# Moving small work between and within the engines' streams in a fused two-block layer: GDN's key decay, its triangles and right side, RG-LRU and mLSTM's second convolution

## What is computed

```python
u = rmsnorm(x, attn_norm) @ w_in          # one product for four mixers
gdn, mlstm, rglru, rwkv = split(u)
y = concat(gated_deltanet(gdn), mlstm(mlstm), rglru_block(rglru), rwkv7_time_mix(rwkv))
x = x + y @ w_out
x = x + swiglu_ffn(rmsnorm(x, ffn_norm))  # 5632 hidden
...                                       # second block: attention, memory, gated merge
```

```python
def gated_delta_rule(q, k, v, g, beta):
    g = jnp.cumsum(g, axis=-1)
    decay = jnp.exp(jnp.where(causal, g[..., :, None] - g[..., None, :], -jnp.inf))
    kb = k * beta[..., None]
    lower = jnp.tril(jnp.einsum('nbhcd,nbhsd->nbhcs', kb, k) * decay, -1)
    rhs = jnp.concatenate([v * beta[..., None], kb * jnp.exp(g)[..., None]], axis=-1)
    sol = lax.linalg.triangular_solve(lower + eye, rhs, ...)
    ...
    k_dec = k * jnp.exp(g[..., -1:] - g)[..., None]
...
def mlstm(...):
    qk = jax.nn.silu(causal_conv(qk, conv_w))        # q and k: two convolutions
...
def rglru_block(u, conv_w, conv_b, w_a, b_a, w_x, b_x, lam):
    xb = causal_conv(xb, conv_w) + conv_b
    r = sigmoid(xh @ w_a + b_a); i = sigmoid(xh @ w_x + b_x)
    log_a = -RGLRU_C * r * jax.nn.softplus(-lam)
```

## Time and profile before

| | us |
|---|---|
| median of 3 runs | 2447.65 |
| lowest, highest | 2445.69, 2447.93 |
| the profiled execution | 2449.26 |
| its span | 2447.5 |
| TensorE busy | 2408.2 (98%) |
| VectorE busy | 1412.7 (58%) |
| ScalarE busy | 1129.1 (46%) |
| GpSimd busy | 113.8 (5%) |
| mean granted clock of TensorE | 0.996 |

### The profile page before, as it was taken

The page is one execution under the profiler, slowest core; times in us unless marked ns, Lnnn a source line. Parts: engine busy times, 40 slices in busy tenths (PEclk is TensorE's granted clock), DMA queues, the critical chain, the costliest instruction groups (busy, mean ns, idle before and its releaser), DMA issues.

```text
span 2447.5 us, 34354 instructions
## 1 busy us (share of the span) xinstructions
PE 2408.2 (98%) x14480; PEld 2050.0 (84%) x14480; DVE 1412.7 (58%) x1834; ACT 1129.1 (46%) x1412; POOL 113.8 (5%) x100
## 2 busy tenths in 40 slices
PE   7999999999999999999999999999999999999998
PEld 7997999987888888888888878898888888888887
DVE  4866657776765555555555565545446645555554
ACT  6535435563454444444434464445444455444444
POOL 2100001210000000000000050000000000000000
PEclk9999999999999999999999999999999999999999
DMA  8633334645555556655555566555545544555564
GB/s 254 211 121 109 134 122 156 220 160 186 193 189 185 187 179 200 194 187 186 179 192 187 187 203 232 184 172 172 161 154 197 170 161 140 199 187 184 195 243 143
DMA packets 225641, 441.53 MB, mean 180 GB/s; under 512 B 11890, under 2 KB 28112, under 8 KB 223056
## 3 DMA queue, kind: packets, MB, share of 16 engines
q1 hardware_dynamic: 221744, 419.80, 52.2%
q0 software_dynamic: 3744, 19.53, 2.1%
HBM read 428.81 MB, written 10.49 MB: 179 GB/s over the span
## 4 chain that ended last, share of the span: by engine, by line
PE 91%; issue 4%; DVE 3%; ACT 2%; DMA 0%; POOL 0%; SPq 0%; ACTq 0%; DVEq 0%; POOLq 0%
PE ps L600 24%; PE ps L601 24%; PE ps L602 24%; PE ps L628 4%; PE ps L629 4%; PE ps L630 4%; PE ps L559 2%; PE ps L1213 1%; PE ps L1202 1%; PE ps L734 1%; DVE ringL L1874 1%; DVE AR L2348 0%; ACT ringH L1274 0%; DMA mem_hold<-memSt 0%; PE ps L818 0%
## 5 line engine op out<-in xcount | busy, mean ns | idle before, releaser
L1274 ACT CAST ringH<-raw 128x1024 fp32r<-128x1024 f32 x780 | 816.1, 1049 | 1008.1 <-PE ps L602 871.0
L1874 DVE TENSOR_TENSOR ringL<-raw,ringH 128x1024 fp32r<-128x1024 f32 x780 | 951.9, 1237 | 442.0 <-ACT ringH L1274 441.1
L600 PE MATMUL ps<-ringH,nS 128*128 128x512 f32 x1376 | 552.6, 402 | 2.3 <-DVE nS L2594 1.1
L602 PE MATMUL ps<-ringH,nS 128*128 128x512 f32 x1376 | 538.0, 391 | 0.0
L601 PE MATMUL ps<-ringL,nS 128*128 128x512 f32 x1376 | 537.8, 391 | 0.0
L628 PE MATMUL ps<-nS,ringH 128*128 128x256 f32 x1056 | 310.4, 294 | 8.4 <-DVE ringL L1874 6.9
L600 PEld LDWEIGHTS ps<-ringH,nS 128*128 128x128 f32 x1376 | 259.3, 188 | 57.2 <-DVE ringL L1874 4.3
L602 PEld LDWEIGHTS ps<-ringH,nS 128*128 128x128 f32 x1376 | 259.0, 188 | 55.5
L601 PEld LDWEIGHTS ps<-ringL,nS 128*128 128x128 f32 x1376 | 259.5, 189 | 49.2 <-issue 0.2
L629 PE MATMUL ps<-nS,ringH 128*128 128x256 f32 x1056 | 300.0, 284 | 0.0
L630 PE MATMUL ps<-nS,ringL 128*128 128x256 f32 x1056 | 299.7, 284 | 0.0
(11 more groups left out here) (413 smaller groups left out, 2135.0 us busy)
## 6 DMA issues: line engine op xcount, KB each, us to landing
raw<-in_w_in SPq DMA_DIRECT2D x189, 1024.0 KB, 5.1
raw<-in_ffn_w_gate SPq DMA_DIRECT2D x44, 1024.0 KB, 5.2
raw<-in_ffn_w_up SPq DMA_DIRECT2D x44, 1024.0 KB, 5.2
raw<-in_ffn_w_down SPq DMA_DIRECT2D x44, 1024.0 KB, 5.1
raw<-in_w_out SPq DMA_DIRECT2D x32, 1024.0 KB, 5.1
raw<-in_w_mem_kv SPq DMA_DIRECT2D x16, 1024.0 KB, 5.2
raw<-in_w_proj_a SPq DMA_DIRECT2D x8, 1024.0 KB, 5.1
raw<-in_w_proj_m SPq DMA_DIRECT2D x8, 1024.0 KB, 5.1
```

The lines of the kernel that those rows point to most:

```text
L600: mm(o, XH[:, ts(j)], WH, first, False)
L602: t_of[0] = mm(o, XL[:, ts(j)], WH, False, last)
L1274: e.copy(ringH[:, h % NSPL, 0:nh * cols], raw[:, u % NRAW, h0 * cols:(h0 + nh) * cols]).then_inc(*hi.tick(h))
L1874: tt2(ringL[:, h % NSPL, o], raw[:, u % NRAW, h0 * cols:(h0 + nh) * cols], ringH[:, h % NSPL, o].bitcast(F32), SUB).then_inc(*lo.tick(h))
```

## The change

It has these parts:

1. `norm` on ScalarE: the root comes one halt earlier.
2. `mem`: TensorE's and VectorE's `factor` for the memory's rows come one halt of one step later.
3. mLSTM's second convolution (q = 1) starts two halts later on TensorE, ScalarE and VectorE.
4. RG-LRU starts two halts later on all engines, GpSimd's products and the transfers of w2s included.
5. The split mix312 becomes mix3, run in one go, and mix1 and mix2, each with a halt after every second chunk. The w_out blocks wait for their own mixer's split.
6. GDN: Kt is scaled by ScalarE (four Copy activations with a scale) in place of VectorE; `pairs` is called for a group when its G is there; the right side of the first chunk is computed within `join`.

```diff
@@ def small_mixers(L):
     while not L.done("r0") and "gdn" not in L.open:
         yield
+    yield
+    yield
     yield from L.stage("rglru")
     yield from L.stage("xload")
...
-    L.run("mix312")
+    L.run("mix3")
     yield
+    for m in (1, 2):
+        for n, _ in enumerate(L.stage(f"mix{m}")):
+            if n % 2:
+                yield
@@ program: gates of the w_out blocks
-                  ("gdn" if m == 2 and q >= 2 else "mix312") if m else "mix0", "V")
+                  "gdn" if m == 2 and q >= 2 else f"mix{m}", "V")
@@ TensorE, mem
                 yield 2
                 yield 2
+                yield 1
                 factor("me", me_p, me_v, rm)
@@ TensorE, mlstm
-                    for _ in range(5):
+                    for _ in range(5 + 2 * q):
                         yield
@@ TensorE, gdn, product vn
                     e.wait_ge(*gd_v.at("R", ch))
+                    e.wait_ge(*gd_v.at("inv", "xt", "j"))
@@ ScalarE, norm
-                yield
                 root(nx_v, nx_a, rx)
+                yield
                 yield
@@ ScalarE and VectorE, mlstm
-                    yield
+                    for _ in range(1 + 2 * q):
+                        yield
@@ ScalarE, gdn
-                yield
-                for _ in range(4):
+                for _ in range(3):
+                    yield
+                Kt = v3(SC + 1024 * 9, 4, 128)
+                e.wait_ge(*gd_a.at("kd"))
+                for h in range(4):
+                    t = act(Kt[:, h, :], Kt[:, h, :], ACT.Copy, scale=kd[:, h:h + 1])
+                t.then_inc(*gd_a.tick("kdt"))
+                for _ in range(2):
                     yield
@@ VectorE, factor
                 e.reciprocal(r, r).then_inc(*mv.tick("r"))
+                if key == "me":
+                    yield
                 e.wait_ge(*mp.at("r"))
@@ VectorE, pairs
-                    first = [(s, bc(mask(C_M1T), 4), bc(ident, 4)) for s in (slice(0, 4), slice(4, 8))]
+                    first = [(s, bc(mask(C_M1T), 4), bc(ident, 4)) for s in (slice(4 * g, 4 * g + 4) for g in groups)]
@@ VectorE, gdn
-                e.wait_ge(*gd_a.at("kd"))
-                for h in range(4):
-                    t = tsc(Kt[:, h, :], Kt[:, h, :], kd[:, h:h + 1], None, MUL)
-                t.then_inc(*gd_v.tick("kd"))
                 yield
...
-                        if w == 0 and g == 1:
+                        if w == 0:
                             own(gd_v)
-                            pairs(("inv",), gd_v, wide, G8, XR8)
+                            pairs(("inv",), gd_v, wide, G8, XR8, (g,))
...
-                yield from join(("inv",), gd_p, gd_v, XR8, T8)
...
+                def right_side(ch, src):
+
+                    own(gd_v)
+                    for h in range(4):
+                        t = tsc(R[:, h, :], src[:, h, :], gcol[:, ch, 4 + h:5 + h], None, MUL)
+                    t.then_inc(*gd_v.tick("R", ch))
+                for n, _ in enumerate(join(("inv",), gd_p, gd_v, XR8, T8)):
+                    if n == 0:
+                        right_side(0, Vt4[:, :, 0, :])
+                    yield
```

More of the change, by code:

```diff
@@ L1252, in tensor @@
                 "norm": norm, "turn": turn_params, "gates": gates, "stat2": stat2, "mem": mem, "rwkv": rwkv, "mlstm": mlstm, "gdn": gdn,
-                "rglru": rglru, "mix312": split(12), "mix0": split(4), **{f"split1.{q}": split1(q) for q in range(4)},
+                "rglru": rglru, **{f"mix{m}": split(4) for m in range(4)}, **{f"split1.{q}": split1(q) for q in range(4)},
                 **{f"split2.{q}": split2(q) for q in range(4)}, "xf": split(8), "attA": attA, "attM": attM, "attB": attB,
@@ L1423, in norm @@
                 yield
+                root(nx_v, nx_a, rx)
                 yield
-                root(nx_v, nx_a, rx)
                 yield
@@ L1845, in scalar @@
                 "gdn": gdn, "rglru": rglru,
-                "mix312": split("mix", nS, lambda k: mix[:, k, :], [*range(12, 16), *range(4, 12)], mix_ready),
-                "mix0": split("mix", nS, lambda k: mix[:, k, :], range(4), mix_ready), "stat1": stat1,
+                **{f"mix{m}": split("mix", nS, lambda k: mix[:, k, :], range(4 * m, 4 * m + 4), mix_ready) for m in range(4)},
+                "stat1": stat1,
                 **{f"split1.{q}": split1(q) for q in range(4)}, "stat2": stat2, **{f"split2.{q}": split2(q) for q in range(4)},
@@ L2076, in mem, with pairs @@
                 yield
-            def pairs(key, mv, of, GT, XTr):
+            def pairs(key, mv, of, GT, XTr, groups=(0, 1)):
                 if of is wide:
-                    first = [(s, bc(mask(C_M1T), 4), bc(ident, 4)) for s in (slice(0, 4), slice(4, 8))]
+                    first = [(s, bc(mask(C_M1T), 4), bc(ident, 4)) for s in (slice(4 * g, 4 * g + 4) for g in groups)]
                 else:
@@ L2485, in gdn @@
                 yield from invert(("inv",), gd_p, gd_v, wide, X8, XR8, T8, 5)
-                yield from join(("inv",), gd_p, gd_v, XR8, T8)
                 R, Sx = v3(SC + 1024 * 4, 4, 128), v3(SC + 1024 * 4 + 512, 4, 128)
                 Vt4 = Vt.rearrange("p (h t) e -> p h t e", t=2)
+                def right_side(ch, src):
[7 more added lines that the diff above has]
+                    yield
                 for ch in range(2):
-                    src = Vt4[:, :, 0, :]
                     if ch:
@@ L2499, in gdn @@
                         tt2(R, Vt4[:, :, 1, :], R, SUB).then_inc(*gd_v.tick())
-                        src = R
-                    own(gd_v)
-                    for h in range(4):
-                        t = tsc(R[:, h, :], src[:, h, :], gcol[:, ch, 4 + h:5 + h], None, MUL)
-                    t.then_inc(*gd_v.tick("R", ch))
+                        right_side(1, R)
                     yield
@@ L2712, in vector @@
                 "norm": norm, "gates": gates, "mem": mem, "rwkv": rwkv, "mlstm": mlstm, "gdn": gdn, "rglru": rglru,
-                "mix312": split("mix", nS, lambda k: mix[:, k, :], [*range(12, 16), *range(4, 12)]),
-                "mix0": split("mix", nS, lambda k: mix[:, k, :], range(4)), "stat1": stat1,
+                **{f"mix{m}": split("mix", nS, lambda k: mix[:, k, :], range(4 * m, 4 * m + 4)) for m in range(4)}, "stat1": stat1,
                 **{f"split1.{q}": scaled_split("x1", xS, "ffn_norm", range(4 * q, 4 * q + 4)) for q in range(4)},
```

## The result

The changed kernel takes 2442.32 us (median of 17 runs, 2440.32 to 2444.55), the kernel before 2447.50 in as many runs beside it (2443.33 to 2449.80): ratio 0.998 with an interval of 0.9973 to 0.9987. It is 5.2 us faster, just at the edge of what I had called a difference, and less than half of the 11 us forecast. The time lies in the range; the size of the gain was wrong.

What follows compares the result with a forecast made beforehand. TensorE, 98% busy, bounds the kernel; 13.7 us of waits and 8.0 of clock were in reach. Terms -1.5 - 3.9 - 5.3 + 2 - 2.7 = -11.4 from 2449.3 gave 2437.9, less 1.6 for the median: 2436.5 us, range 2430 to 2446.

Steps and rivals of the forecast that it cites:

- First norm: TensorE's 1.47 us wait for the norm's reciprocal goes, as the root runs in ScalarE's idle time: -1.5 us.
- Memory's factor: At L662 near 120 us, the 2.38 us wait and 1.6 of half clock go: -3.9 us.
- mLSTM's convolution: At L963 near 200 us, 3.07 of wait and 3.2 of clock go, 1.0 comes at L835: -5.3 us.
- GDN's start: RG-LRU's tiny chain beside GpSimd's products: 6.1 us go, new waits of 3.4 and 2.6 plus 1.6 clock come: +2.
- Kt on ScalarE: Four scalings (2.76 us) leave VectorE for ScalarE copies, which stay hidden: nothing of its own.
- Rest of GDN: Inversion and splits: waits of 0.80, 1.12, 0.71 and 1.6 of clock go, 1.5 given back: -2.7 us.
- The clock: Half-speed stretches after four waits or wait groups cost 1.6 + 3.2 + 1.6 + 1.6 = 8.0 us, taken as recoverable.
- the third: Rival, whole kernel: the waits go but the clock doesn't come back; -5 us, 2442.6; chance 0.08.
- The second: Rival: GpSimd holds VectorE twice as long, GDN's start costs 10 instead of 2; -3.4 us, 2444; chance 0.14.
- Slower: Rival: from 440 to 620 us every GpSimd product stands in VectorE's way; +6.4 us, 2454; chance 0.06.

Runs made afterwards that it cites:

- part 6 alone: Kernel before with only Kt decayed by ScalarE, pairs by group and right side within the join: 2444.83 us, ratio 0.9987.
- part 4 by itself: Kernel before with only RG-LRU two halts later, Kt still scaled by VectorE: 2452.30 us, ratio 1.0018.
- parts 3 or 4 alone: Two runs on the kernel before: only mLSTM's second convolution two halts later, 2445.27 us; only RG-LRU two halts later, 2452.30 us.

## Why the prediction was wrong in its size

The sum of -11.4 us held 5.5 of waits and 5.9 of clock. Of the waits 2.0 came. Of the clock came 3 to 4. Two steps failed: the account of which edit ends which wait, above all in the rest of GDN, and the price in clock put on each wait. By its own steps, each from the positions of the same work in the two profiled executions:

*First norm,* -1.5: -1.5. Right; the root comes in ScalarE's idle time, and no cast came late enough for TensorE to wait.

*Memory's factor,* -3.9: -4.2 in the traces, of which 2.4 is the wait. Right in the mechanism. The 1.6 of clock was there in the first profile of before and not in the second.

*mLSTM's convolution,* -5.3: -4.0. The new wait for the reciprocal, taken as 1.0, was 0.94. What I missed is a second one of 0.95 for ringL at 227. ScalarE's and VectorE's timelines show how the first came about:

```profile
207.98 0.42 ACT L1600 ACTIVATE AR<-AR 128x256 f32<-128x256 f32 x1 [2.44 <-DVE AR L2365]
...
208.42 1.28 ACT L1504 ACT_TABLE_LOAD   x1
...
209.72 0.21 ACT L1504 ACTIVATE small<-small 128x8 f32<-128x8 f32 x1
...
210.88 1.28 ACT L1600 ACT_TABLE_LOAD   x1
...
206.43 1.52 DVE L2365 SCALAR_TENSOR_TENSOR AR<-AR,prm 128x256 f32<-128x256 f32 x3
...
209.96 0.20 DVE L2187 RECIPROCAL small<-small 128x8 f32<-128x8 f32 x1 [1.93 <-ACT small L1504]
```

The SiLU of a chunk ends, the root's table is loaded (1.28), and 1.2 us on the SiLU's again (1.28). The load is followed by its activation within 0.02 us, so the smaller price of a switch was the right one in this chain. (The 2.66 us of the Trainium skill, "ScalarE: Activation LUTs", section "What ACT_TABLE_LOAD costs", would have given a wait of 2.3; the trace has 0.94.)

*GDN's start,* +2: +3.3, inside the bounds. The mechanism was as written, and close in size: waits of 3.4 and 2.6 forecast, 4.19 and 2.38 measured. The prediction had the operations with two inputs wait for 3.15 us in all; held were two operations, one of them with a single input, for 3.7 us. The second half of ringL, taken as 1.2, took 2.64 beside L2824. The second clock fall came as well. (This is the contention which the Trainium skill, "GPSIMD Engine Reference", section 8, states for VectorE instructions with two SBUF inputs or in a 2-port performance mode. L2565 has two inputs. L2559 has a single one by its row and was held all the same, for 1.0 us; whether it ran in such a mode no trace shows.)

*Kt on ScalarE,* nothing: right. Its four copies took 1.28 us at 500.07 in the trace of the change, and nobody waited for them. But the 2.76 us that the prediction took off VectorE were for the most part GpSimd's hold, which moved on to a half of ringL, as part 6 alone has shown.

*Rest of GDN,* -2.7: -0.7. The step of the waits that failed most by size. I gave 1.5 us back for RG-LRU's second half beside the inversion's levels, without a place for it. What was in fact late stands in the timelines of GpSimd and VectorE: RG-LRU's first half, which moved behind the last group of G.

```profile
504.27 2.40 POOL L2764 TENSOR_TENSOR AR<-AR 128x1024 f32<-128x1024 f32 x1 [2.65 <-ACT AR L1343]
...
508.76 2.41 POOL L2852 TENSOR_TENSOR AR<-AR 128x1024 f32<-128x1024 f32 x1
...
511.14 1.72 POOL L2829 TENSOR_TENSOR AR<-AR 128x512 f32<-128x512 f32 x1
...
509.80 1.92 DVE L2590 SCALAR_TENSOR_TENSOR AR<-AR 128x512 f32<-128x512 f32 x1 [5.96 <-ACT AR L1748]
...
511.76 1.40 DVE L2592 TENSOR_SCALAR AR<-AR 128x512 f32<-128x512 f32 x1
...
513.67 2.35 DVE L1889 TENSOR_TENSOR ringL<-raw,ringH 128x1024 fp32r<-128x1024 f32 x2
```

VectorE stood idle for 5.96 us until ScalarE's L1748, then its two operations (1.92 and 1.40) ran beside GpSimd's products, and ringL, ready for making since 510.7, came behind them: 1.67 us. And the waits of 0.80 and 1.12, which I had counted as gone, are both there, for a level operation and for mix3. The change leaves the level operations as they are. Of the splits it cuts what was run in one go behind mix3, not mix3's own four; and the wait of 1.12 had never been for twelve subtractions, as the prediction read it. In VectorE's timeline of the kernel before they read

```profile
573.83 4.11 DVE L2594 TENSOR_TENSOR nS<-AR,nS 128x256 fp32r<-128x256 f32 x12 [2.42 <-ACT nS L1744]
```

and L600 started at 574.40, 0.57 us behind the first of them and 3.5 before the last was done. What was late was the first, for which VectorE had waited 2.42 us on ScalarE. I should have asked of each wait which edit ends it.

*The clock,* -8.0 within these terms, and 2.1 put back. This is the other failed step: "Gone: ... 1.6 of half clock", written beside four of the waits as if it were their price. One profiled execution has shown 8.5 us, another 1.7, with the same waits. The runs say what a mean execution has: mean granted clock 0.9966 over 57 runs of before, 0.9978 over the 17 of the change, so (0.9978 - 0.9966) x 2447 = 2.9 us, where 5.9 was forecast. Together with 2.0 us of waits this makes 4.9 of the measured 5.2. That it fits so well is partly luck. The mean takes in the last microseconds of the program, where the clock is low in every trace and TensorE is done, at no cost: 0.8 and 1.4 us of loss in the two traces of before, 2.2 and 2.3 in those of the change. Without them the clock gave some 4 us by this estimate, and the two together 6 for the measured 5.2: the split is not exact to a microsecond. I had also read a hint and passed over it: the profiled execution was 1.6 us above the median, one fall of the clock.

Sum of waits by the prediction: 14.0 gone (the 0.3 of L1145 among them), 1.0 + 3.4 + 2.6 + 1.5 new, 5.5 us less. Measured: 2.0 less. The difference is 0.95 at 227, 0.8 - 0.2 at GDN's start, and 2.1 behind it.

Of the rivals, the third, in which the waits go and the clock does not come back, was the nearest in number (2442.6), and half for its reason: a third to a half of the clock's 5.9 us did not come, but more than half of the waits' 5.5 us stayed too, so its nearness is in part luck. The second (2444) had GpSimd holding VectorE, which is so, but with 10 us at GDN's start for the measured 3.3. *Slower* was real for part 4 by itself, at 4.5 us.

## What to carry to other kernels

Work that needs nothing but parameters belongs where the engines are idle, not at the head of the stage that uses it: here moving a chain of tiny operations gave 8 us on top of the change, more than the whole change had. Before moving a step by some halts on all engines, lay its place on GpSimd beside VectorE's in the new order, and count a VectorE operation that meets a GpSimd product at work as waiting for its end, as these traces show it for operations from 128x4 to 128x1024. Taking the held operation away does not take the hold away, if another comes in its place. And price waits and clock separately: take the waits from a trace, where they repeat to 0.05 us, but the clock from the mean of many runs.

## What the runs showed of the hardware

A VectorE operation on 128x4, four elements in each partition, waits out a GpSimd product: 1.20 and 2.89 us for 0.17, both ending within 0.04 us of it. Beside the product cut to 128x8 the second took 0.16. Scalings with one tensor as input are held as well (Kt's four, 2.76 us for some 0.8). It goes the other way too: GpSimd's L2824 took 3.38 us, where the same product (L2806 at 485.58) had taken 2.36 in the kernel before; it began at 478.21, while a ringL operation (478.13, 1.22 us, not held) was at work.

The granted clock falls to 0.50 for 3 to 4 us at a time, a loss of 1.7 us where TensorE is busy (1.70 or 1.71 in each of the sums with one fall), and two such in a row lose 3.4. Where it falls isn't fixed by the program. The same wait of 2.37 us at 121 had a fall behind it in the first profile of before and with part 6 alone, and none in the second or with parts 3 or 4 alone. What decides it the runs leave open.
